# Two transformer blocks on one core: layer-norm edges handed over tile by tile, idle-filling zero products dropped there

## The reference

```
x = _layer_norm(alpha * x + 0.5 * _swiglu(x, ffn_w_gu[l, 0], ffn_w_down[l, 0]), ln_g[l, 0], ln_b[l, 0])
mix = _token_mixers(x, w_in[l], ...)     # four kinds of attention, 20 heads' units, ends in @ w_out
x = _layer_norm(alpha * x + mix, ln_g[l, 1], ln_b[l, 1])
x = _layer_norm(alpha * x + 0.5 * _swiglu(x, ffn_w_gu[l, 1], ffn_w_down[l, 1]), ln_g[l, 2], ln_b[l, 2])
```

## Time and profile before

| | us |
|---|---|
| median of three runs | 1995.51 (1994.26 to 1997.62) |
| the profiled execution's own time | 1997.44 |
| its span, first to last instruction | 1995.6 |
| PE busy | 1738.1 (87%) |
| DVE busy | 890.6 (45%) |
| ACT busy | 640.8 (32%) |
| POOL busy | 163.5 (8%) |
| mean granted TensorE clock | 0.922 |

### The profile page before, as it was taken

One profiled execution on the slowest core, in us unless ns is written; L12 is line 12 of the kernel. 1 busy time (PEld: TensorE's weight loads), 2 busy tenths in 40 slices (PEclk: granted clock), 3 DMA queues, 4 the chain that ended last, 5 costly groups with the idle time before them and its releaser, 6 DMA issues.

```text
span 1995.6 us, 30411 instructions
## 1 busy us (share of the span) xinstructions
PE 1738.1 (87%) x11864; PEld 1353.8 (68%) x11864; DVE 890.6 (45%) x1277; ACT 640.8 (32%) x906; POOL 163.5 (8%) x129
## 2 busy tenths in 40 slices
PE   6998878767777677899989889999999989889997
PEld 5776666523333223599967678999799967769996
DVE  3557333201111111455555736554655555655555
ACT  5324332111111111333323434443333323434442
POOL 2212220000000000000022300000000022310000
PEclk9998989878887778899999989999999999899998
DMA  9440225699999999865434025535544433045510
GB/s 401 149 159 32 85 85 211 256 426 425 426 425 426 426 426 426 328 252 189 171 145 148 1 90 213 184 124 209 195 177 168 186 124 127 1 169 189 189 63 21
DMA packets 53183, 421.44 MB, mean 211 GB/s; under 512 B 6496, under 2 KB 7264, under 8 KB 8416
## 3 DMA queue, kind: packets, MB, share of 16 engines
q1 hardware_dynamic: 51360, 409.08, 52.0%
q10 hardware_dynamic: 1728, 11.03, 1.5%
HBM read 419.03 MB, written 1.05 MB: 211 GB/s over the span
## 4 chain that ended last, share of the span: by engine, by line
issue 65%; PE 25%; DVE 5%; POOL 4%; ACT 2%; DMA 0%; DVEq 0%; POOLq 0%; ACTq 0%
PE bank L1398 10%; PE bank L799 6%; PE bank L809 3%; PE bank L1444 2%; POOL small L483 1%; PE bank L1462 1%; POOL ring_r L439 1%; DVE xTl L465 1%; PE bank L1453 1%; ACT ring_r L433 1%; PE bank L1439 1%; DVE ring_r L439 0%; PE bank L1362 0%; PE bank L981 0%; DVE lg L1532 0%
## 5 line engine op out<-in xcount | busy, mean ns | idle before, releaser
L882 DVE TENSOR_TENSOR wl<-ring,wh 128x2048 fp32r<-128x2048 f32 (+1 forms) x176 | 308.9, 1759 | 252.9 <-ACT wh L839 252.9
L799 PE MATMUL bank<-xh,wh 128*128 128x256 f32 x1408 | 398.7, 283 | 7.9 <-DVE wl L882 7.9
L799 PE MATMUL bank<-xh,wl 128*128 128x256 f32 x1408 | 397.8, 283 | 0.0
L799 PE MATMUL bank<-xl,wh 128*128 128x256 f32 x1408 | 397.8, 283 | 0.0
L839 ACT ACTIVATE wh<-ring 128x1024 fp32r (+3 forms) x176 | 252.6, 1485 | 202.8 <-PE bank L809 202.8
L799 PEld LDWEIGHTS bank<-xh,wh 128*128 128x128 f32 x1408 | 269.2, 191 | 13.5 <-DVE wl L882 9.8
L799 PEld LDWEIGHTS bank<-xl,wh 128*128 128x128 f32 x1408 | 269.3, 191 | 3.8
L799 PEld LDWEIGHTS bank<-xh,wl 128*128 128x128 f32 x1408 | 269.4, 191 | 0.0
L1398 PE MATMUL bank<-ring_r,xTh 128*128 128x512 f32 (+1 forms) x736 | 216.8, 402 | 16.1 <-DVE xTl L465 9.5
L1398 PEld LDWEIGHTS bank<-ring_r,xTh 128*128 128x128 f32 x736 | 142.9, 195 | 51.6 <-DVE xTl L465 10.8
L548 PE MATMUL bank<-ring,xg 128*32 128x256 f32 x1664 | 130.4, 458 | 47.2 <-DMA ring<-in_we 44.6
(11 more groups left out here) (274 smaller groups left out, 2299.9 us busy)
## 6 DMA issues: line engine op xcount, KB each, us to landing
...
```

The costliest lines, as they stand in the source:

```text
L799: ins = pe.matmul(bank[4 + p][:, m * S:(m + 1) * S], w[p][:, cols], v[:, k], start=(k == 0 and n == 0), stop=(k == KD - 1 and n == 2))
L882: dve.tensor_tensor(wl[p][:, cols], ring[:, bass.ds(ring_tile(t) + cols.start, n)], wh[p][:, cols].bitcast(F32), ALU.subtract).then_inc(wl ...
```

## The change

- The loop over layers is written out. x is no longer scaled by ALPHA ahead of a norm; the first DVE operation of the norm computes x·(ALPHA/scale) + bank, and eps is divided by scale².
- The last two `down` tiles of an FFN, and the last chunk of a projection, are ordered by bank, and each bank's end is posted (`f_bk`, `w_bk`). DVE adds and takes statistics bank by bank, and POOL gets the two tiles' variances one after the other, each of width 1.
- Tile 0 is normalized on ACT (`act_norm`), tile 1 on DVE in two halves; g and b are not applied there but after the transposes, on ACT, as scale and bias of a partition (`act_norm_T`, from `gcol`, made once of `grows` by a transpose in the routing). DVE then makes high and low from `xf`. g and b are applied to x itself later on POOL (`pool_affine`, eight operations of 128x512).
- PE transposes each tile as it is ready. All of `pe_keep(…, 28)` around norms goes, also the 12 around the clearing of the banks and the 8 ahead of the input projection; 4 stay after the experts. The next stage starts with the first pair of blocks (`up_first`, and `tb` in `pe_part`). `up_first` does the products with `xl` last.
- The first tile's high and low parts are made ahead of the norm (`act_first`, `dve_first`), those of the second tile on ACT and POOL (`act_second`, `pool_second`). `whu`/`whd`/`wlu`/`wld` replace `wh`/`wl`.
- The first FFN tiles are issued as the experts' slots come free, chunk by chunk. The experts' last sums are posted by bank (`m_bk`). The experts' loop itself is unchanged.
- For the output projection POOL's high part of chunk 0 waits for `t_src`, the scaled heads of the differential attention (L1211), and ACT's of chunk 1 for the last unit's values instead of its scores.
- The result leaves in two transfers, a tile each.

```diff
-                    ins.then_inc(m_sc, 1)
+                            ins.then_inc(m_bk if i + c < 2 else m_sc, 1)
...
+            act_first(act, 0)
...
-            dve.wait_ge(m_sc, last + 2)
+            dve_first(dve, 0)
             for i in range(NT):
                 for c in range(2):
+                    if i + c < 2:
+                        dve.wait_ge(m_bk, last * 3 + (2 * i + c + 1))
+                    else:
+                        dve.wait_ge(m_sc, last + 2)
                     ins = dve.tensor_tensor(x[:, i, c * 512:(c + 1) * 512], bank[2 * i + c][:],
                                             x[:, i, c * 512:(c + 1) * 512], ALU.add)
-                    if i + c < 2:
-                        st.then(ins)
-            st.sync()
-            ins.then_inc(x_ok, 1)
+                    if c == 0:
+                        st.link(ins)
+                ins.then_inc((x0_ok, x_ok)[i], 1)
...
                     for v in range(FSLOTS):
-                        if f == 0:
-                            sp.wait_ge(wl_ok, g * FFN_W + (2 * last_tile[v] + 2))
+                        if g == 0:
+                            sp.wait_ge(e_used, last_pair * (2 * TURN) + max(
+                                j + 1 for j in range(2 * TURN) if e_slot[j % ESLOTS] in chunks_in(v)))
...
+        def act_first(act, g):
+            tile_landed(act, g, 0, 0)
+            ffn_high(act, g, 0, 0, False)
+
+        def act_second(act, g):
+            tile_landed(act, g, 0, 1)
+            ffn_high(act, g, 1, 1, False)
+
+        def act_high_down(act, g):
+            if g >= 1:
+                act.wait_ge(f_dn, g * (FT + 1))
+            ffn_high(act, g, 0, 0, True)
+
+        def pool_second(pool, g):
+            pool.wait_ge(wl_ok, (g + 1) * FFN_W + 1)
+            pool.wait_ge(wh_ok, g * FFN_W + 2)
+            ffn_low(pool, 1, 1, False, pre_ok)
...
+        def pool_affine(pool, st, j, after):
+
+            pool.wait_ge(*after)
+            pool.wait_ge(t_ps, NORM_T[j] + 4)
+            pool.wait_ge(ln_in, (j + 1) * 16)
+            for i in range(NT):
+                for c in range(2):
+                    cols = slice(c * 512, (c + 1) * 512)
+                    st.then(pool.tensor_tensor(x[:, i, cols], x[:, i, cols], ln[:, 0, cols], ALU.mult))
+            st.sync()
...
+            ins.then_inc(xp_ok, 1)
...
+        def clear_sums(pe):
+            for b in range(4):
+                ins = pe.matmul(bank[b][:], zeros[:, 0:P], zeros[:], start=True, stop=False, skip_group_check=True)
+            ins.then_inc(f_dn, 1)
+
+        def pe_norm_T(pe, j, tb, clear=False):
+
+            for i in range(NT):
+                for b in range(KD):
+                    if i == 0 and b == 0:
+                        pe.wait_ge(x0_ok, 4 + j)
+                    if i == 1 and b == 0:
+                        pe.wait_ge(pow_ok, POW1 + j // 3 * POW2 + (2, 6, 8)[j % 3])
+                        if clear:
+                            clear_sums(pe)
+                        pe.wait_ge(xc_ok, j + 1)
+                    if i == 1 and b == KD // 2:
+                        pe.wait_ge(x_ok, 4 + j)
+                    ins = pe.transpose(bank[4 + b // 2][:, (b % 2) * S + i * P:(b % 2) * S + (i + 1) * P],
+                                       x[:, i, b * P:(b + 1) * P], ident[:])
+                    if i == NT - 1 and b % 2 == 1:
+                        ins.then_inc(t_ps, 1)
...
+            def up_first():
+
+                pe.wait_ge(wl_ok, g * FFN_W + FFN_W + 1)
+                if g == 0:
+                    pe.wait_ge(t_out, tb + 1)
+                for low_x in (False, True):
+                    for m in range(2):
+                        for k in range(KD):
+                            if m == 0 and k % 2 == 0:
+                                if low_x:
+                                    pe.wait_ge(t_out, tb + (k // 2 + 1))
+                                else:
+                                    pe.wait_ge(xh_ok, xb + (k // 2 + 1))
+                            cols = slice(k * 2 * P + m * P, k * 2 * P + (m + 1) * P)
+                            for w, v in (((whu, xl),) if low_x else ((whu, xh), (wlu, xh))):
+                                ins = pe.matmul(bank[4][:, m * S:(m + 1) * S], w[0][:, cols], v[:, k],
+                                                start=(not low_x and m == 0 and k == 0 and w is whu), stop=False,
+                                                skip_group_check=True)
...
+            for b in range(3):
+                down_into(FT - 2, 0, b)
+            down_ready(FT - 1)
+            for b in range(3):
+                down_into(FT - 1, 1, b, f_bk)
+            down_into(FT - 2, 0, 3, f_dn)
+            down_into(FT - 1, 1, 3, f_dn)
...
+            j = l * 3 + 2 * f
+            if j > 0:
+                act.wait_ge(xp_ok, j)
+            load_ln(act, j)
+            if f == 0:
+                act_high(act, run2(l, 0), 0)
             silu(FT - 2, 0)
             down_free(FT - 2)
-            high(FT - 1, 1, True)
+            ffn_high(act, g, FT - 1, 1, True)
+            if f == 1 and l < LAYERS - 1:
+                act_first(act, g + 1)
             silu(FT - 1, 1)
+            if f == 1 and l < LAYERS - 1:
+                act_second(act, g + 1)
+                act_high_down(act, g + 1)
+                act_norm(act, st, l * 3 + 2)
...
-            st.then(dve.tensor_scalar(x[:], x[:], ALPHA, None, ALU.mult))
...
+            if f == 1 and l < LAYERS - 1:
+                dve_first(dve, g + 1)
             hidden(FT - 1, 1)
...
+        def norm_sums(dve, st, j, scale, waits, between=None):
 
             st.sync()
...
+            if j > 0:
+                dve.wait_ge(xp_ok, j)
+            for b in range(4):
+                i, c = b // 2, b % 2
+                part = x[:, i, c * 512:(c + 1) * 512]
+                dve.wait_ge(*waits[b])
+                st.link(dve.scalar_tensor_tensor(part, part, ALPHA / scale, bank[b][:], ALU.mult, ALU.add))
+                st.then(dve.bn_stats(bn[:, i, c], part))
+                if c == 1:
+                    st.sync()
+                    st.link(dve.bn_aggr(mean[:, i], bn[:, i].rearrange("p c k -> p (c k)")))
+                    if i == 0:
+                        st.then(dve.tensor_scalar(nmean, mean[:, 0, 0:1], -1.0, None, ALU.mult))
+                        st.sync()
+                    dve.tensor_scalar(rs[:, i:i + 1], mean[:, i, 1:2], 1.0, EPS2 / scale ** 2, ALU.mult, ALU.add)\
+                       .then_inc(var_ok, 1)
+
+        def layer_norm(dve, st, j, scale, waits):
+
+            norm_sums(dve, st, j, scale, waits)
+            dve.wait_ge(pow_ok, norm_pow(j) + 1)
+            for c in range(2):
+                part = x[:, 1, c * 512:(c + 1) * 512]
+                dve.tensor_scalar(part, part, mean[:, 1, 0:1], rs[:, 1:2], ALU.subtract, ALU.mult)\
+                   .then_inc((xc_ok, x_ok)[c], 1)
+
+        def act_norm(act, st, j):
+
+            act.wait_ge(pow_ok, norm_pow(j))
+            st.link(act.activation(nmr, nmean, ACT.Copy, scale=rs[:, 0:1]))
+            act.activation(x[:, 0], x[:, 0], ACT.Identity, bias=nmr, scale=rs[:, 0:1]).then_inc(x0_ok, 1)
+
+        def act_norm_T(act, j, tb):
+
+            act.wait_ge(gcol_ok, 1)
+            for k in range(KD):
+                if k % 2 == 0:
+                    act.wait_ge(t_ps, tb + (k // 2 + 1))
+                ins = act.activation(xf[:, k], bank[4 + k // 2][:, (k % 2) * S:(k % 2 + 1) * S], ACT.Identity,
+                                     bias=gcol[:, j, 1, k:k + 1], scale=gcol[:, j, 0, k:k + 1])
+                if k % 2 == 1:
+                    ins.then_inc(xf_ok, 1)
...
+            def top(q):
+                dve.wait_ge(xf_ok, j * 4 + q + 1)
+                dve.tensor_copy(pair(high, q), pair(xf, q)).then_inc(xh_ok, 1)
+
+            def rest(q):
+                dve.wait_ge(xh_ok, j * 4 + 4 + q + 1)
+                dve.tensor_tensor(pair(xl, q), pair(xf, q), pair(high, q).bitcast(F32), ALU.subtract).then_inc(t_out, 1)
+
...
-                pe.wait_ge(t_out, tb + 19)
-                pe_part(pe, run2(l, 1), 0, xTl2, 0)
-                pe_ffn(pe, l, 1, tokens)
+                pe_part(pe, run2(l, 1), 0, xTh, xl, 0, tb + 15, w_bk)
+                pe_ffn(pe, l, 1)
...
-                act.wait_ge(sc_ps, (l + 1) * UNITS2 + UNITS1)
+                act.wait_ge(pv_ps, (l + 1) * UNITS2 + UNITS1)
...
+                pool.wait_ge(t_src, l * 2 + 6)
                 pool.wait_ge(t_ps, tb + 15)
                 pool.wait_ge(d_land[run.slots[0]], run.lands[0])
...
+                g = l * 2 + 1
+                pool_second(pool, g)
+                for i in range(NT):
+                    pool.wait_ge(var_ok, l * VAR2 + (VAR1 + 5 + i))
+                    inverse_root(pool, rs[:, i:i + 1])
...
+                if tb is not None:
+                    pe.wait_ge(t_out, tb + (c - first + 1))
...
+                    for i in range(NT):
```

(8 more changed lines are left out.)

414 lines of the change are left out of this document (236 added, 178 removed).

## The result

| | before | after |
|---|---|---|
| median of the runs (range) | 1994.9 us (1991.7 to 1997.6) | 1935.2 us (1933.8 to 1935.7) |
| span of the profiled execution | 1995.6 | 1932.0 |
| ratio | | 0.970, 95% interval 0.968 to 0.972 |

What follows compares the result with a forecast made beforehand. PE bounds each stage, so its time without useful work between stages counts. Terms 13.2 + 7.2 + 4.8 + 8.3 + 8.0 + 3.0 + 1.5 = 46.0 us off 1997.44 give 1951.4, stated as 1950; range 1940 to 1963, with rivals 1932 to 1972.

Steps and rivals of the forecast that it cites:

- the third rival: Five norms and unit 13: no clock loss and all of the stall back, 11.5 + 3.6 us more, 1935; chance 0.12.
- Norm 0: Edge from `down` to input projection, twice: 17.1 us becomes 8.9; with clock terms 6.6 gained each, 13.2 in all.
- Norms 1 and 2: Edges into FFNs: norm 1 gains 3.6 us, twice 7.2; norm 2 of layer 0 gains 4.8.
- POOL's power of 1.74 us: In each norm, POOL's power operation on a tile's variance was taken to last 1.74 us.
- 2.3 us for each norm edge: Clock loss at each norm edge: PE idles without zeros, so the next stage starts at half clock; 2.3 us.
- the waits between pairs: FFN start behind norm 1: stalls between pairs of transposed blocks in `up_first` were to cost 0.3 us.
- Experts' edge: Experts to FFN 0: earlier tiles and fewer zeros let PE start sooner, gaining 8.3 us; bounds 3.5 and 10.
- Unit 13: Attention, twice: the cast waits for L1211, whose products fall to about 0.9 us; 4.0 us each, 8.0; bounds 0 and 5.8.
- Output projection: Its start, twice: it follows the second `xTl` and not the eighth, about 1.5 us each, 3.0 in all.
- End: Program end: sums start earlier and half the bytes follow, gaining 1.5 us; bounds 0.5 and 2.5.
- The first: Rival at projections and FFN starts: through the shared port `pool_affine` delays DVE's low parts, 15 us, 1965; chance 0.15.
- The fourth: Rival at the norms: without zeros PE stays at half clock far into each stage, 2014 at 30 us each; chance 0.03.

Runs made afterwards that it cites:

- zeros_back: The changed kernel with products of zeros put back on TensorE at the five norm edges; 1929.8 us.
- b_no_zeros: The kernel before without its zeros at the norm edges and ahead of the first FFN, nothing else changed; 2001.5 us.
- both_k_outer: The changed kernel with zeros back at the norms, nmax scaled on ACT and the m and k loops of `up_first` swapped; 1914.3 us.
- tiles_late: The changed kernel, but the tiles of FFN 0 are asked for only when the last expert chunk is used; 1942.5 us.
- both experiments on the cast: GpSimd's cast no longer waits for VectorE's scaling of cat in the changed kernel, 1948.3 us; that wait added to the kernel before, 1987.4 us.
- both_tail: both_k_outer with 3 products of zeros ahead of the values of the last four attention units; 1911.6 us.

## Why the prediction was right or wrong, by its steps

The measured 1935.2 lies below the forecast's own range (1940 to 1963), and inside the stated 1932 to 1972 only because that one takes in the third rival. Every term of the sum has the sign that was forecast; the sizes were wrong at norms 1 and 2 and at the output projection.

- **Norm 0: right in its total, in part by luck.** Gap 8.6 us for 8.9 in layer 0, 8.3 in layer 1. Two errors cancel in it. The first power ends at T + 1.5 for T + 2.6, being 1.2 us shorter than forecast. But ACT is in chunk 0's high part until 1009.17 (L452, which the prediction does not have), 0.6 us behind the power's result, and from tile 1 (T + 5.6 for T + 6.5) to the first product it takes 3.0 us for 2.4. The clock fell as said (2.3 us): 3.0 lost in layer 0, 1.9 in layer 1; zeros_back gives it back. Where else it falls is chance, as the prediction had it: the kernel before lost 1.5 us in the projection of layer 0 behind a wait near 1080, the changed one did not; in that of layer 1 it fell once more in both (for 3.4 us from 1663.5 and from 1615.7).
- **Norms 1 and 2: mechanism right, size wrong.** 14.4 us came from the two norms 1 with the FFNs behind them for 7.2, and 8.0 from norm 2 for 4.8. By the bounds, 7 for a norm 1 and 7.4 for norm 2, one norm 1 (7.7) and norm 2 lie outside. Two terms failed. "POOL's power of 1.74 us": it takes 0.56. (At norm 1 the prediction has its end at T + 2.5, though 0.3 and 1.74 make 2.0. POOL's low part ends at T + 0.2, as said, and the power at T + 0.8.) The 1.74 of the earlier trace rows seems to have been a wait itself: in the kernel before it starts 0.1 us behind a VectorE operation with two inputs in SBUF (two of them in the row, 1.24 each):

```profile
1023.28 2.48 DVE L933 SCALAR_TENSOR_TENSOR x<-x,small,ln 128x1024 f32<-128x1024 f32 x2
```

  A second reason would be the width: the power was over 128x2 and is now 128x1. The same trace settles how much that is. In the first block, where no VectorE operation runs beside it, a power over 128x2 takes 0.70 us all eight times:

```profile
175.91 0.70 POOL L483 TENSOR_TENSOR small<-small,minus_half 128x2 f32<-128x2 f32 x1
```

  So some 1.0 of the 1.2 us is the wait, and 0.15 the width. In the new order sums out of PSUM and statistics stand beside the power. It takes 0.55 or 0.56 us at every norm but for the second power at the program's end, where such an operation runs again and it takes 1.52:

```profile
1923.96 2.47 DVE L1132 SCALAR_TENSOR_TENSOR x<-x,small,ln 128x1024 f32<-128x1024 f32 x2
```

  The Trainium skill (SBUF — State Buffer, "Who interferes with whom") says that a VectorE instruction with two SBUF inputs contends with a GpSimd instruction that reads SBUF; these rows agree, with 1.70 to 1.74 us beside one at the norms before and 0.70 without. It is read from the traces, not tested alone.

  The other failed term is "2.3 us for each norm edge": at norms 1 and 2 the clock was back before `up` began, and cost 0.9 us of the edge at norm 1 of layer 0, 0.8 at norm 2 and nothing at norm 1 of layer 1 (against the same edges in zeros_back). b_no_zeros measures 2.3 where the edge is 15 us long. Against this, the waits between pairs cost 1.2 us and not 0.3; both_k_outer gives 0.75 of it back.
- **Experts' edge: right,** 8.7 us for 8.3 in these traces, and tiles_late shows that 5.3 of it are the early tiles: they landed before 809.7, not near 812. That the 28 zeros no longer hold up the transposes is worth some 2.2 more, by the edge in b_no_zeros (10.5 us for 12.8). From the experts' first product to FFN 0 the kernel before took 464.6 us, its two variants 462.0 and 461.8, the nine kernels with early tiles 455.7 to 456.7 (the changed one 456.0): 5.8 to 8.7 is what the change brings.
- **Unit 13: right, and above its bound.** The stall fell by 4.3 us (4.0 forecast), as both experiments on the cast confirm: one wait for VectorE, and nothing else, moves it. The other 1.7 of the 6 us is clock, at half for 13.7 us where it was 17.1 before; the bound of 5.8 left the clock out.
- **Output projection: wrong by size,** 0.3 us for 3.0, below its bound of 0.5 for each layer. In both_k_outer and both_tail, where the clock is at full there, its first product is 3.1 us behind the transposes' first (4.9 before): 1.8, the 1.5 that was meant. In the changed kernel half clock reaches into these transposes (16 take 3.47 us, 1.96 before) and takes most of it.
- **End: right,** 2.0 for 1.5. **First block: not in the sum.** It was 3.1 us shorter by chance: the same instructions bring the experts' first product to anywhere from 360.7 to 366.0 us in the three kernels with the old edges (363.4 in the mean), and from 362.6 to 369.1 in the six that share the changed kernel's first block (365.0). No gain shows in that, and a loss of a us or two is not excluded.
- **Rivals.** The first has its mechanism right and its price wrong. Beside `pool_affine` VectorE's low parts do take longer: six of the 84 of FFN tiles 2.50 to 2.96 us for 2.29, and three of projection chunks 3.07 to 3.30, the very sign that the prediction named as "wrong":

```profile
1586.27 3.30 DVE L458 TENSOR_TENSOR ring_r<-ring,high 128x2048 fp32r<-128x2048 f32 x1 [2.50 <-ACT high L452]
```

  PE waits for none of them: its one long wait inside the input projection of layer 0 (2.27 us, at 1060.43) stood in the kernel before as well (2.30, at 1078.88), and what the FFNs behind a norm lose, 1.2 us, is lost at their first pairs. The 15 us of the rival are nowhere. The third gave the time, 1935, but half by its reasons: the clock took nothing on balance (54.6 us at half behind the experts in both traces), while 4.9 us went to it at the two norms 0, a stall of 1.7 us stayed, and the shorter power is in no rival. That its number was met is luck. The fourth's mechanism is real (124.5 us at half in b_no_zeros) and was far from its turning point.

As a whole, the 46.0 of the sum became 63.6 between the two traces and 59.6 between the medians. Of the 17.6 more, 10.4 stand at norms 1 and 2, 4.1 at unit 13, 3.1 are chance, 1.9 norm 0, 0.9 the experts and the end, and the output projection took 2.7 back.
